# A 256-token transformer kernel on one core: a column-wise start, another borrowed weight buffer in the RWKV block, key norms in strips

## The reference, cut to what matters

```python
def rmsnorm(x, g):
    y = xf * lax.rsqrt(jnp.mean(xf * xf, axis=-1, keepdims=True) + RMS_EPS)
    return (y * g)
def swiglu(h, w_gate, w_up, w_down):
    return (jax.nn.silu(h @ w_gate) * (h @ w_up)) @ w_down
x = x + 0.5 * swiglu(rmsnorm(x, norm_ffn1), w_ffn1_gate, w_ffn1_up, w_ffn1_down)   # f1
# RWKV: keys normed by head (12 heads of 64), and a bonus
kk = kk * lax.rsqrt(jnp.maximum(jnp.sum(kk * kk, axis=-1, keepdims=True), 1e-24))
bonus = jnp.sum(r * k * r_k, axis=-1, keepdims=True) * v
y = (out + bonus) * g
```

## Time and profile before

| | |
|---|---|
| median of 3 runs | 1584.71 us (1584.13 to 1586.28) |
| the profiled execution | 1583.54 us, span 1582.2 us |
| TensorE (PE) busy | 1552.2 us, 98% |
| VectorE (DVE) busy | 1046.7 us, 66% |
| ScalarE (ACT) busy | 864.7 us, 55% |
| GpSimd (POOL) busy | 131.9 us, 8% |
| 16 DMA engines, mean | 180 GB/s |

### The profile page before, as it was taken

How to read it: one execution, slowest core, us unless ns; L and a number is a source line. 1 busy time by engine, 2 the same in 40 slices (tenths; PEclk the granted TensorE clock), 3 DMA queues, 4 the chain that set the end, 5 groups by cost and what they waited for, 6 DMA issues and landing times.

```text
span 1582.2 us, 26450 instructions
## 1 busy us (share of the span) xinstructions
PE 1552.2 (98%) x11150; PEld 1355.0 (86%) x11150; DVE 1046.7 (66%) x1501; ACT 864.7 (55%) x1270; POOL 131.9 (8%) x126
## 2 busy tenths in 40 slices
PE   7999999999999999999999999999999999999998
PEld 7888898688888988889988888888888888898886
DVE  5556676766566665668975775667765676776566
ACT  6455556655555555556753364555555565655553
POOL 0000020000000010002564001000110010001000
PEclk9999999999999999999999999999999999999999
DMA  7997556246655466555310366553755542455652
GB/s 281 232 270 267 196 170 247 82 175 219 205 186 187 158 215 208 173 194 183 129 52 4 135 216 210 176 195 131 252 203 191 186 172 95 163 209 187 203 174 76
DMA packets 42185, 285.08 MB, mean 180 GB/s; under 512 B 4926, under 2 KB 4942, under 8 KB 10196
## 3 DMA queue, kind: packets, MB, share of 16 engines
q1 hardware_dynamic: 39024, 272.29, 49.4%
q0 software_dynamic: 3040, 11.12, 3.2%
HBM read 277.62 MB, written 5.24 MB: 179 GB/s over the span
## 4 chain that ended last, share of the span: by engine, by line
PE 46%; DVE 2%; ACT 1%; issue 1%; DVEq 0%; ACTq 0%
PE P L239 44%; PE P L250 1%; ACT whi L213 0%; DVE wlo L227 0%; PE P L2237 0%; DVE AR L379 0%; DVE AR L2338 0%; DVE AR L2346 0%; DVE xt L2834 0%; DVE sm L2101 0%; DVE x L367 0%; DVE AR L2756 0%; DVE AR L2795 0%; DVE AR L2762 0%; DVE x L390 0%
## 5 line engine op out<-in xcount | busy, mean ns | idle before, releaser
L239 PE MATMUL P<-xt,whi 128*128 128x512 f32 (+1 forms) x3264 | 725.5, 346 | 3.7 <-ACT whi L213 1.6
L239 PEld LDWEIGHTS P<-xt,whi 128*128 128x128 f32 x3264 | 559.4, 191 | 73.6 <-issue 6.7
L227 DVE TENSOR_TENSOR wlo<-raw,whi 128x2048 fp32r<-128x2048 f32 x245 | 559.4, 2290 | 51.3 <-PE P L239 46.4
L213 ACT ACTIVATE whi<-raw 128x2048 fp32r<-128x2048 f32 x245 | 467.5, 1909 | 145.2 <-PE P L239 81.8
L239 PE MATMUL P<-xt,wlo 128*128 128x256 f32 x2544 | 439.7, 282 | 0.0
L239 PEld LDWEIGHTS P<-xt,wlo 128*128 128x128 f32 x2544 | 386.8, 191 | 17.8
L619 DVE SCALAR_TENSOR_TENSOR AR<-P,AR 128x256 f32<-128x256 f32 x228 | 96.4, 423 | 244.2 <-ACT AR L612 244.1
L239 PE MATMUL P<-whi,hh 128*128 128x512 f32 x504 | 197.5, 392 | 0.0
L239 PE MATMUL P<-wlo,hh 128*128 128x512 f32 x504 | 196.8, 390 | 0.0
L239 PE MATMUL P<-whi,hl 128*128 128x512 f32 x504 | 196.1, 389 | 0.0
L612 ACT ACTIVATE AR<-P 128x256 f32<-128x256 f32 x228 | 85.6, 375 | 118.4 <-PE P L239 118.1
(11 more groups left out here) (236 smaller groups left out, 1024.2 us busy)
## 6 DMA issues: line engine op xcount, KB each, us to landing
raw<-ws SPq DMA_DIRECT2D x249, 1024.0 KB, 4.9
gb<-gains SPq DMA_DIRECT2D x14, 512.0 KB, 7.3
by_distance<-AR POOLq DMA_DIRECT2D x8, 512.0 KB, 7.4
AR<-by_distance POOLq DMA_DIRECT2D x1, 2048.0 KB, 19.0
AR<-by_distance POOLq DMA_DIRECT2D x1, 1536.0 KB, 10.0
x<-x_in SPq DMA_DIRECT2D x2, 512.0 KB, 4.2
AR<-mem_in POOLq DMA_DIRECT2D x1, 1024.0 KB, 5.5
AR<-gains SPq DMA_DIRECT2D x2, 512.0 KB, 4.7
```

Of the source, the lines that this page charges most:

```text
L213: act.e.activation(k.whi[n % NHI][:, :], k.raw[u % NRAW][:, :], ACT.Copy).then_inc(*k.s_hi.inc(u))
L227: dve.e.tensor_tensor(k.wlo[n % NLO][:, :], k.raw[u % NRAW][:, :], k.whi[n % NHI][:, :].bitcast(F32), ALU.subtract).then_inc(*k.s_lo.inc(u))
L239: return pe.e.matmul(o, l, r, start=start, stop=stop, skip_group_check=True)
```

## The change

- **Start.** A new input `x_col` holds the f1 gains and x turned, by 128-column tiles. SP loads it in two halves, then units 0 and 1 in half units with the two halves of the tokens between, then unit 2. TensorE runs 18 products of ones first. ScalarE makes the high parts of x as copies scaled by the gain, VectorE the low parts. The lead takes all 256 tokens at once. The factor 1/rms of a token comes later: it is broadcast over the partitions by a product with a diagonal matrix (`RROW`) and multiplied into every gate sum of f1 (`rooted_vector`, 22 times), and it scales the sum of f1 when that is added to x.
- **f1's order** is g0 g1 g2 g3 d0 g4 ...; four banks for gate sums; high parts in its first units one later.
- **The other FFNs**: in the first three places the high part for three units on is made after the chain, not before.
- **Distance table**: its product stands in the start; 16 writes of a quarter megabyte, each behind one more used unit; reads in four and two pieces.
- **Lent buffer**: that of U_RWKV + 10 (the query unit). The two others take the six units that follow (`raw_of`, `raw_before`).
- **Key norms**: the sums go to three strips of 32 partitions, two heads pairs a strip, in the order 0, 2, 4, 1, 3, 5; the spreads read three strips of 32 rows in the same order.
- **Where parts are made**: in RWKV's inputs no more low parts of U+11 and U+12 and no high of U+12; high U+12 and both low parts after the turns of k and b; high U+13 and U+14 after the U0 copies; high of f4's first unit before the last high part of the heads; f4's second and third high parts together after the first norm.

```diff
+def raw_of(u):
+    return (u if u < U_BORROWED + 3 else u + 1 if u < U_BORROWED + 5 else u + 2) % NRAW
+def raw_before(u):
+    if U_BORROWED + 3 <= u < U_BORROWED + 7:
+        return u - 2
+    return U_BORROWED if u == U_BORROWED + 7 else u - NRAW
-U_BORROWED = U_RWKV + 12
+U_BORROWED = U_RWKV + 10
...
+        if t == "f1" and j == 0:
+            order += [("g", 2), ("g", 3), ("d", 0)]
...
+def rooted_vector(k, dve, t, f, part):
+    dve.wait_ge(*k.s_ea.after("rrow"))
+    dve.wait_ge(*k.s_dv.after("gate sum", f))
+    dve.e.tensor_tensor(part, part, k.RROW, ALU.mult).then_inc(*k.s_tt.inc(t, f, 0))
...
-    banks = (6, 4, 5) if t == "f1" else (6, 7, 4, 5)
+    banks = (6, 7, 4, 5)
...  ffn_scalar
-        if n < len(ORDER) - 1:
+        if t == "f1" and n < 3:
+            hi_to(k, act, u + 2)
+        elif 3 <= n < len(ORDER[t]) - 1:
             hi_to(k, act, u + 3)
...  after the high part of the hidden values
+            if t != "f1" and n < 3:
+                hi_to(k, act, u + 3)
...  bias_pool
-    for i in range(8):
-        if i:
-            pool.wait_ge(*k.s_hf.after("f1", 2 + i))
+    for i in range(16):
+        pool.wait_ge(*k.s_used.after(U_FFN1 + 3 + i))
...
+NORM_ORDER = (0, 2, 4, 1, 3, 5)
+NORM_STRIP = {j: (j // 2, j % 2) for j in NORM_ORDER}
-        return mm(pe, P[5][0:12, 0:NT], k.SEL[:, 12 * j:12 * j + 12], k.SQ[:, j, :], j == 0, j == 5)
+        g, turn = NORM_STRIP[j]
+        return mm(pe, P[5][32 * g:32 * g + 32, 0:NT], k.SEL[:, 32 * j:32 * j + 32], k.SQ[:, j, :], turn == 0, True)
...
+    for j in NORM_ORDER:
+        n, i = divmod(j, 2)
+        r = slice(32 * NORM_STRIP[j][0], 32 * NORM_STRIP[j][0] + 32)
+        last = mm(pe, P[1 + n][:, i * NT:(i + 1) * NT], k.SPREAD[r, 128 * j:128 * j + 128], k.NRM[0][r, :])
...  rwkv_inputs_scalar, rwkv_inputs_vector
-        hi_to(k, act, U + 10 + n)
+        hi_to(k, act, U + 10 + min(n, 1))
-        lo_to(k, dve, U + 10 + n)
+        lo_to(k, dve, U + 10)
...  rwkv_products_scalar, rwkv_products_vector, at the end
-    hi_to(k, act, U_RWKV + 14)
+    hi_to(k, act, U_RWKV + 12)
+    lo_to(k, dve, U_RWKV + 12)
...  rwkv_chunks_scalar, after the U0 copies; after root(1)
+    hi_to(k, act, U_RWKV + 14)
+    hi_to(k, act, U_FFN4)
...  sync_program
+    sp.e.dma_start(k.XCOL[:, 0:1032], k.x_col[:, 0:1032]).then_inc(*k.s_col[0].inc(by=16))
+    sp.e.dma_start(k.XCOL[:, 1032:2056], k.x_col[:, 1032:2056]).then_inc(*k.s_col[1].inc(by=16))
+    part(0, 0)
+    part(0, 1)
+    tokens(0)
+    part(1, 0)
+    tokens(1)
+    part(1, 1)
+    load_units(k, sp, 2, NRAW)
-    load_units(k, sp, U_RWKV + 16, U_RWKV + 17)
-    load_units(k, sp, U_RWKV + 15, U_RWKV + 16)
-    load_units(k, sp, U_RWKV + 17, U_FFN4 + 6)
+    load_units(k, sp, U_RWKV + 15, U_FFN4 + 6)
...
+def warm_tensor(k, pe):
+    pe.wait_ge(*k.s_po.after("one"))
+    for n in range(18):
+        mm(pe, k.P[7][:, 0:128], k.ONE, k.ONE)
 def begin_tensor(k, pe):
+    warm_tensor(k, pe)
+    for u in range(3):
+        for s in range(2):
+            begin_high_tensor(k, pe, u, s)
+        if u == 1:
+            distances_tensor(k, pe)
+            for a in range(2):
+                pe.wait_ge(*k.s_dv.after("diag", a))
+                last = mm(pe, k.P[7][:, 128 * a:128 * a + 128], k.ONE, k.DIAG[:, a, :])
+            last.then_inc(*k.s_pe.inc("rrow"))
+        for s in range(2):
+            last = begin_low_tensor(k, pe, u, s)
+        last.then_inc(*k.s_used.inc(u))
+    pe.wait_ge(*k.s_ev.after("dist"))
+    pe.wait_ge(*k.s_ea.after("rrow"))
...  begin_scalar: scaled high parts of x and quarters of unit 0, in turn
+    for c in range(6):
+        high(c)
+    part(0, 0, 0, 1)
+    for c in range(6, 8):
+        high(c)
+    part(0, 0, 1, 2)
+    part(0, 1, 0, 1)
+    part(0, 1, 1, 2)
+    square(0)
+    part(1, 0, 0, 2)
+    square(1)
+    part(1, 1, 0, 2)
```

More of the change, by code:

```diff
@@ L148, in tiles_and_signals @@
     k.s_gn = [sig("gn0"), sig("gn1")]
+    k.s_col = [sig("col0"), sig("col1")]
+    k.s_part = [[sig(f"part{u}{s}") for s in range(2)] for u in range(2)]
     k.s_id, k.s_vec, k.s_cst, k.s_base, k.s_rel = (
@@ L222, in lo_to @@
             n = SPLIT_NO[u]
[L223 removed]
+            dve.wait_ge(*k.s_raw[raw_of(u)].after(u))
             if n >= NLO:
@@ L343, in scalar @@
         k, t = self.k, self.t
[L344 to L348, removed]
+        for h in range(2):
+            act.wait_ge(*k.s_res.after(t, a, h))
         if self.free is not None:
@@ L3169, in begin_scalar, with high @@
     act.e.activation(k.sm[:, 31:32], k.sm[:, 30:31], ACT.Sqrt)
-    for a in range(2):
-        k.norm["f1"].scalar(act, a)
-    turn_scalar(k, act, "f1", None, FIRST, (4, 5))
-    hi_to(k, act, U_FFN1 + 1)
-    turn_scalar(k, act, "f1", None, SECOND, (6, 7))
-    hi_to(k, act, U_FFN1 + 3)
+    def high(c):
+        act.wait_ge(*k.s_col[c // 4].after())
+        act.wait_ge(*k.s_col[0].after())
+        act.e.activation(k.xt[:, c, :, 0, :], k.XRAW[:, c, :, :], ACT.Copy,
+                         scale=k.GCOL[:, c:c + 1]).then_inc(*k.s_xh.inc("f1", c))
@@ new lines, in begin_vector @@
+    for c in range(8):
+        dve.wait_ge(*k.s_xh.after("f1", c))
+        dve.e.scalar_tensor_tensor(out=k.xt[:, c, :, 1, :], in0=k.XRAW[:, c, :, :], scalar=k.GCOL[:, c:c + 1],
+                                   in1=k.xt[:, c, :, 0, :].bitcast(F32), op0=ALU.mult,
+                                   op1=ALU.subtract).then_inc(*k.s_xl.inc("f1", c))
+    low(0, 0)
+    low(0, 1)
+    low(1, 0)
+    for a in range(2):
+        dve.wait_ge(*k.s_sq.after("f1", a))
+    dve.e.tensor_scalar(k.sm[:, 10:12], k.sm[:, 4:6], 1.0 / DM, 1e-6, ALU.mult, ALU.add).then_inc(*k.s_var.inc("f1"))
@@ new lines, in begin_vector @@
+    dve.wait_ge(*k.s_rt.after("f1"))
+    dve.e.reciprocal(k.sm[:, 10:12], k.sm[:, 6:8]).then_inc(*k.s_dv.inc("f1", "rstd"))
+    dve.wait_ge(*k.s_id.after())
+    dve.wait_ge(*k.s_dv.after("f1", "rstd"))
+    for a in range(2):
+        dve.e.tensor_scalar(k.DIAG[:, a, :], k.cs[:, C_ID:C_ID + 128], k.sm[:, 10 + a:11 + a], None,
+                            ALU.mult).then_inc(*k.s_dv.inc("diag", a))
+    dve.e.tensor_scalar(k.sm[:, 12:14], k.sm[:, 10:12], 0.5, None, ALU.mult).then_inc(*k.s_dv.inc("f1", "half"))
@@ L3185, in begin_vector @@
+    low(1, 1)
+    dve.lo = U_FFN1 + 2
+    distances_vector(k, dve)
     lo_to(k, dve, U_FFN1 + 2)
```

232 lines of the change are left out of this document (137 added, 95 removed).

## The result

| | before | after |
|---|---|---|
| median of 5 runs | 1585.38 us (1584.13 to 1586.75) | 1579.43 us (1577.21 to 1580.43) |
| the profiled execution, its span | 1583.54, 1582.2 | 1577.21, 1575.9 |

The ratio is 0.9967, with a 95% interval of 0.9956 to 0.9978: faster by 5.2 us (5.9 between the medians), where 9.5 was forecast (1575.2). The time is inside the range of 1571 to 1580, the size is off by some 4 us.

The account below looks back on a forecast made before the run. TensorE was taken as the bound, busy 1552.2 of 1582.2 us. Terms -4.2 - 0.8 - 2.5 - 0.9 + 0 - 1.1 = -9.5 gave 1574.0 for the profiled execution, 1575.2 as median; range 1571 to 1580.

Parts of the forecast that it names:

- Behind the keys' turn: Before the inverse: one high and two low parts moved into VectorE's idle time, hidden, 0 us; bounds -0.4 and +2.5.
- the port lock: Rival, chance 0.11: VectorE's low parts and GpSimd's masks for the inverse block each other, costing 1 to 2.5 us; 1577.
- a GpSimd operation of over 4 us: Sign that the forecast is wrong: a POOL operation this long around 813 us, at the inverse's masks.
- half a start: Rival, chance 0.16: the changed start gives half, unit 7 starting at 54 instead of 51.9; 1577.3 us.
- Start: Kernel start: x sent already turned and multiplied at once, dummies against the low clock; -4.2 us, bounds -6.2 and -1.5.
- First FFN: First FFN: smaller bias-table writes and four PSUM banks remove one TensorE stall; -0.8 us, bounds -0.9 and +1.5.
- "slower" rival: Rival, chance 0.04: 22 bias pieces in the first FFN delay weight loads, costing 19 us against 9.5; 1594.
- Key norms: RWKV inputs: six sums and six spreads overlap in three strips, 1.0 us each; -2.5 us, bounds 0 and -3.5.
- Strips don't overlap: Rival, chance 0.06: the key-norm products in strips run one after another, 0 of the 2.5 us gained; 1577.7.
- Bonus wait: RWKV inputs: v's turn no longer waits for the first bonus, two low parts moved away; -0.9 us, bounds -0.9 and +0.5.
- After the RWKV: FFN behind the RWKV: TensorE's wait for the third high part goes; -1.1 us, bounds -1.1 and 0.
- Moved high parts: Other FFNs: the fifth unit's high part goes behind gate 1's chain, no effect; 5 x 0.5 if the cover went.

Follow-up runs that it names:

- e1: Changed kernel with both loads of the last two output units held until the middle of the inverse, near 829 us; 1576.41 us, ratio 0.9946.
- e2: Changed kernel with both of those loads held until the first U0 products, near 855 us; 1577.80 us, ratio 0.9963.
- e4: Changed kernel with one of the two loads left at 809 us and the other held to 818 us; 1576.50 us, ratio 0.9950.
- e5: e4 with GpSimd's work on the bonus moved later; 1574.64 us, ratio 0.9939.
- e9: Changed kernel with the two loads apart, at 829 and 846 us, and GpSimd's bonus work later; 1574.89 us, ratio 0.9936.
- e8: e4 without the 18 dummy products of ones at the start; 1579.55 us, ratio 0.9969.
- e7: e4 without the strips, key-norm sums and spreads made as in the kernel before; 1579.15 us, ratio 0.9967.
- e12: e9 with the high parts ahead of the chain again in the five other FFNs; 1575.54 us, ratio 0.9936.
- e3: Kernel before with two unused 1 MB copies, device memory to device memory, issued near 818 us; 1591.81 us, ratio 1.0049.

## Why the prediction was off by four microseconds

- **The step that failed** is "Behind the keys' turn ... Hidden, at **0**; bounds -0.4 and +2.5". It measured +5.1 in the profiles, twice the upper bound. Three things are in it. *Not seen at all*, 3.3 us: the queues. It is what e1, e2 and e4 don't lose in this stretch (they lose 1.7 to 1.8), with the loads elsewhere or apart. The prediction said of the loads that "their slots are free by the same low parts" and asked only whether they would be in time. It did not ask what their new moment would hit: from 789 to 799 of before, beside products of 256 columns, TensorE had no wait on "issue"; at 809 to 817 the loads met its small products, which use up a packet of instructions in 3.4 to 4 us. *Foreseen as a rival*, 1.0 us: the port lock, 1.8 in e4 against 0.8 in e5 (forecast 1 to 2.5); its sign, a GpSimd operation of over 4 us, showed: 5.09 at 806.65 in the changed kernel. *Left over*, 0.8: e9 has no load near and no second collision (a mask still holds its first low part), and yet the wait of 0.94 on "issue"; what makes it is open. Nor did the inverse start earlier, as the bound of -0.4 had it: the changed kernel is 8.98 ahead at 802.28 and 8.99 at 814.75.
- **The range** holds the time by luck: its upper end, 1580, came from half a start and the port lock together, and what happened is neither. Two slips in the sums change nothing: 56.2 less 51.9 is 4.3, and the two terms of the lower end give 1572.2, so that 1571 goes further and leaves nothing out.
- **Start**, -4.2 forecast, -3.3 measured. Each piece is close: first products 8.45 (8.7), unit 3 behind a wait of 1.6 (1.5), then 0.72 and 0.85 (0.8, 0.95) against the earlier trace rows. Unit 3 began at 28.87 instead of 28.0, and that is the 0.9. It waits for a chain on VectorE and ScalarE: the low part of unit 2 began at 19.93 (19.3 in the sum), because VectorE first waited for the distances product and copied it (L1164, 19.32), a step that the sum had only on TensorE. Gate 0's chain then ended at 24.5 (23.8), the high part of unit 3 at 26.3 (25.7), its low part at 28.7 (28.0). TensorE's units 0 to 2 took 18.8 us against 17.8, but it waited 1.47 behind them. The dummies did what they were for: 1.7 in e8's profile.
- **First FFN**, -0.8 forecast, -0.9 measured; the stall of the earlier trace rows is gone, and no new one in its place. The 22 multiplications and the 22 pieces stayed hidden; the "slower" rival is out.
- **Key norms**, -2.5 forecast, -2.2 in the profile and 2.7 in e7 (perhaps with a spell of low clock), but from other parts than I said, so the sum is right partly by luck. The sums gained 0.4, not 1.7: TensorE did two, then waited 0.65 for the squares, where the earlier trace rows had one run of 12 records. The spreads gained 1.7 and began as soon as the reciprocal was out, with no wait for it, where the forecast had one. "Strips don't overlap" is out: 12 records take 1.07, against 2.78.
- **Bonus wait**, -0.9 forecast, -1.2 measured from start to start.
- **After the RWKV**, -1.1 forecast, -1.5 measured; the earlier trace rows's wait is gone.
- **Moved high parts**, 0 forecast, none seen (e12).
- With the two causes in the inverse taken out (e9) the ratio is 0.9936; the forecast's was 0.9940. The other five terms add up to -9.1, against -9.5. That e9 comes so near is partly luck: the 0.9 of the start and the 0.8 left in the inverse are made up by stretches without a term, 0.6 of the -1.4, the -0.6 behind the inverse (three waits on "issue" of 1.3 before, one of 0.7 after) and the -0.3 at the end.

What stays open: why a stand pulls the clock down for 6.8 us once, 3.4 another time and not at all a third time; how a load holds the packet back, since the traces show when a packet ran and not since when it was asked for; and what makes the wait of 0.7 to 0.9 us on "issue" near 816 to 821 that the changed kernels have, in e1, e2 and e9 with no load near.

## What to carry to other kernels

Small matrix products use up the instruction stream fast enough that its own transfers become a supply to plan for: here 16 KB each 3.4 to 4 us. Keep megabyte loads away from such stretches, or put them where TensorE waits for others anyway (e9). One load at a time is not enough by itself (e8). When a step is moved that frees a buffer, look at where the load it releases will fall, not only at whether it comes in time; and when a wait has "issue" as its end, look at the instruction queue's packets before blaming an engine.

## What the runs showed of the hardware

- A stand of TensorE without any semaphore, 2.2 to 4.3 us, in six traces, each where an instruction packet fell due within 1 MB transfers beside products of 64x64. Where TensorE waited for other engines meanwhile, a late packet made none (e9: 832.93, 5.8 us behind the last). In the six TensorE went on 2.4 to 2.8 us after the packet's start (815.38 to 817.76, 860.30 to 862.72, 827.97 to 830.52, 818.03 to 820.48, 813.79 to 816.19, 825.02 to 827.78).
- Transfers into SBUF (after, 3.0 us) and into device memory (e3, 4.3 us) both do it.
- The Trainium skill, "Advanced Engine Details and Errata", section "ISA Cache", has lines of 16 KB, which are 256 instructions; the trace agrees: 253 products and weight loads for each of the 88 packets of the kernel before.
- The low clock behind a stand can cost nearly as much as the stand: 2.2 us beside 2.9 (after). It began within 0.6 us of TensorE's going on (818.28, 863.30, 830.47, 820.70).
